# Weight sums of the third projection pair moved to VectorE, and the projection work reordered, in a DeltaNet layer step

## The reference, cut to what matters

```python
h = rmsnorm(x, norm1_g) * (1 + scale1) + shift1
proj = h @ w_in                       # columns: pool, q, k, v, gate, beta, alpha, merge
qkv = silu(short_conv(proj[..., OFF_Q:OFF_G], conv_w))   # 5 taps, depthwise
q, k = l2norm(q) * DN_HEAD_DIM ** -0.5, l2norm(k)
o_f, s_f = gated_delta_chunked(q, k, v, beta_f, g_f, s0_f)     # 8 heads of 128
o_b, s_b = gated_delta_chunked(flip(q), flip(k), ...)          # the other direction
o = rms(o_f + flip(o_b)) * onorm_g * silu(gate)
x = x + gate1 * ((merge_a * a_out + merge_b * (o @ dn_proj)) @ w_out)
```

## Time and profile before

| | us |
|---|---|
| median of 3 runs | 2573.36 (2573.13 to 2573.65) |
| profiled execution, its own time | 2571.28 |
| its span in the profile | 2569.5 |
| prologue, up to `scan_done` of L1377 | 129.8 |
| eight heads, up to the last L1358 | 129.8 to 1353.1 |
| output projection, routing and experts | 1353.1 to 2569.5 |

### The profile page before, as it was taken

One profiled execution on the slowest core, in us unless ns is written; L12 is line 12 of the kernel. 1 busy time (PEld: TensorE's weight loads), 2 busy tenths in 40 slices (PEclk: granted clock), 3 DMA queues, 4 the chain that ended last, 5 costly groups with the idle time before them and its releaser, 6 DMA issues.

```text
span 2569.5 us, 39903 instructions
## 1 busy us (share of the span) xinstructions
PE 2370.0 (92%) x14256; PEld 1718.9 (67%) x14256; DVE 1122.5 (44%) x2133; ACT 943.5 (37%) x2447; POOL 440.5 (17%) x295
## 2 busy tenths in 40 slices
PE   6889899898989989897999999959999999999998
PEld 3456556465655556565564444549999999999996
DVE  2657585765758576674623531770100100010013
ACT  3154555536455553644431113312223223222313
POOL 0222231322323132232310000000110011011000
PEclk8989999999999999998999999979999999999999
DMA  9610202011010201102224332266788788878874
GB/s 325 233 44 20 65 26 73 17 39 58 21 65 25 74 17 39 44 10 65 68 94 173 112 130 98 91 220 217 237 285 300 251 276 289 292 239 287 298 246 157
DMA packets 198401, 361.05 MB, mean 141 GB/s; under 512 B 8954, under 2 KB 72327, under 8 KB 195243
## 3 DMA queue, kind: packets, MB, share of 16 engines
q1 hardware_dynamic: 192139, 341.77, 38.0%
q0 software_dynamic: 6176, 18.29, 2.8%
HBM read 319.97 MB, written 40.06 MB: 140 GB/s over the span
## 4 chain that ended last, share of the span: by engine, by line
PE 52%; DVE 2%; issue 1%; DMA 1%; ACT 1%; POOL 0%; SPq 0%; DVEq 0%; ACTq 0%; POOLq 0%
PE bank L2373 20%; PE bank L2387 10%; PE bank L2002 5%; PE bank L1739 4%; PE bank L729 3%; PE bank L1757 2%; PE bank L710 1%; PE bank L2011 1%; PE bank L2345 1%; PE bank L2355 1%; PE bank L926 0%; PE bank L718 0%; DMA arena<-in_w_in 0%; PE bank L2413 0%; PE bank L995 0%
## 5 line engine op out<-in xcount | busy, mean ns | idle before, releaser
L729 PE MATMUL bank<-arena 128*128 128x512 f32 x1344 | 697.4, 622 | 21.6 <-ACT arena L763 21.6
L2373 PE MATMUL bank<-arena 128*128 128x144 f32 x4096 | 512.9, 286 | 3.1 <-ACT arena L2421 3.1
L2373 PEld LDWEIGHTS bank<-arena 128*128 128x128 f32 x4096 | 509.6, 190 | 3.2 <-ACT arena L2421 3.2
L2488 DVE TENSOR_TENSOR arena<-arena,bank 128x144 f32<-128x144 f32 x128 | 39.1, 306 | 698.2 <-ACT arena L2435 698.2
L729 PEld LDWEIGHTS bank<-arena 128*128 128x128 f32 x1344 | 221.9, 195 | 119.4 <-issue 95.0
L2387 PE MATMUL bank<-arena 128*128 128x144 f32 x2048 | 257.3, 286 | 0.7 <-DVE arena L2488 0.7
L2387 PEld LDWEIGHTS bank<-arena 128*128 128x128 f32 x2048 | 253.8, 189 | 1.9 <-DVE arena L2488 0.9
L1101 ACT ACTIVATE arena<-bank 128x384 f16<-128x384 f16 (+1 forms) x360 | 163.7, 492 | 215.1 <-PE bank L918 118.4
L2435 ACT ACTIVATE arena<-bank 128x144 f32<-128x144 f32 x128 | 37.4, 292 | 464.3 <-PE bank L2373 464.3
L926 PEld LDWEIGHTS bank<-arena 128*128 128x128 f16 x1296 | 98.7, 98 | 149.8 <-issue 127.4
L1186 DVE SCALAR_TENSOR_TENSOR arena<-arena 128x1156 f32<-128x1156 f32 x96 | 143.1, 1490 | 0.3
(11 more groups left out here) (311 smaller groups left out, 3185.2 us busy)
## 6 DMA issues: line engine op xcount, KB each, us to landing
arena<-in_exp_w_gate SPq DMA_DIRECT2D x32, 2048.0 KB, 10.1
arena<-in_exp_w_up SPq DMA_DIRECT2D x32, 2048.0 KB, 14.9
arena<-in_exp_w_down SPq DMA_DIRECT2D x32, 2048.0 KB, 10.8
arena<-in_w_in SPq DMA_DIRECT2D x52, 512.0 KB, 5.2
arena<-in_ada_w SPq DMA_DIRECT2D x24, 1024.0 KB, 7.9
side_dram<-arena SPq DMA_DIRECT2D x20, 576.0 KB, 5.7
arena<-g_dram SPq DMA_DIRECT2D x16, 576.0 KB, 4.3
arena<-in_x_sample SPq DMA_DIRECT2D x16, 512.0 KB, 7.1
```

What stands on the lines that cost most here:

```text
L729: ins = nc.tensor.matmul(bank[:, 0:LH], w[:, k, :], x[:, k, :], start=(k == 0 and job[2] in "127"), stop=(k == KH - 1), skip_group_check=( ...
L2373: last = nc.tensor.matmul(banks[3 + f % 2][:, m * CAP:(m + 1) * CAP], w_unit[2 * half + m][:, k, col:col + P], xsT[:, k, :], start=(k == 0 ...
```

## The change

- **Order of the jobs in the loop**: the context jobs of qv and kg come first (qvc0, qvc1, kgc0, kgc1), then the other seven of qv, the other seven of kg, then AB as before. In the last head job g2 moves from before CD to between CD and EF, and the DMA of `w_dn[0]`, which waits for g2, moves behind the waits for CD3 on SyncE.
- **Units of fill**: "start" 5 to 4; "Y20", "Y21", "Y22" from 1.5, 1.5, 1 to 1, 0.5, 0.5; the last group's product place in the first three levels (P2_2, P4_2, P8_2) 1 to 0; "fix" 3 to 4; "end1" 4 to 5.5. With the sum of the rest in "end2", 14.25 units follow the last scan step where 9.25 did. In the last head only the three places P2_2, P4_2, P8_2 change, to 0.
- **ScalarE** copies the jobs of "start" between the SiLU of q and that of v, ahead of the table load and of the wait for `scan_done`.
- **GpSimd** makes, right behind `scan_done`, the sums 1, 2 of qv, 1, 2, 4 of kg and 3 of qv and kg, then the masks L1427 and L1434, then sum 4 of qv. The kg sums have space of their own (`w_sum2`, over part of the masks and prologue tables), so they needn't wait for qv's jobs.
- **VectorE** makes the four AB sums of the seven loop heads in the scan: two behind the tap of chunk 2, one in chunk 4, one in chunk 7. In the last head GpSimd makes them.
- **Taps**: order v, q, k in place of q, v, k. Levels 4 and 8 have none now; one each stays in levels 16, 32, 64; 12 lie in the scan (10 before), with two in chunk 3 and one behind the state of chunk 5.
- **Prologue**: the last token sum `h_sum3` on GpSimd waits for `scan_done`; TensorE no longer waits for it.

```diff
-        ORDER = pair_jobs("qv") + pair_jobs("kg") + pair_jobs("AB")
-        ORDER_LAST = pair_jobs("AB") + ("g0", "g1", "g2") + pair_jobs("CD") + pair_jobs("EF")
+        (QV_C, QV_X), (KG_C, KG_X) = split("qv"), split("kg")
+        ORDER = QV_C + KG_C + QV_X + KG_X + pair_jobs("AB")
+        ORDER_LAST = pair_jobs("AB") + ("g0", "g1") + pair_jobs("CD") + ("g2",) + pair_jobs("EF")
...
-        FILL = {"start": 5, "nk": 2.75, "qT": 4, "kk": 4, "Y20": 1.5, "Y21": 1.5, "Y22": 1, "X0": 1, "X1": 1, "X2": 1, "res": 2, "fix": 3, "end1": 4}
-        FILL |= {f"{x}{b}_{g}": 1 for b in LEVELS for x in "ZP" for g in range(3)}
+        FILL = {"start": 4, "nk": 2.75, "qT": 4, "kk": 4, "Y20": 1, "Y21": 0.5, "Y22": 0.5, "X0": 1, "X1": 1, "X2": 1, "res": 2, "fix": 4, "end1": 5.5}
+        FILL |= {f"{x}{b}_{g}": 0 if b in LEVELS[:3] and (x, g) == ("P", 2) else 1 for b in LEVELS for x in "ZP" for g in range(3)}
...
             silu(1)
             silu(0)
+            evac("start")
             silu(2)
             act.preload_act_table_set(LN_EXP)
             act.wait_ge(sem("scan_done"), h + 1)
-            evac("start")
...
+            def sums_fourth(pair):
+                one, to = weights_of(pair[0]), sums_of(pair)
+                if pair != "kg":
+                    eng.wait_ge(sem("pj_filled"), job_at(h, order, pair + "2"))
+                sum_out(pair + "4", to[2], one[:, KH:KD, :], to[1], ALU.subtract)
...
-                if not last_h and lv > 0:
-                    conv_tap(dve, h + 1, 0, lv - 1)
+                if lv >= 3:
+                    tap()
...
+            sums_first, sums_third, sums_fourth = sum_steps(dve, nc.vector, h, order)
+            tap()
             remainder(1)
             tap()
             state(0)
...
             for t in range(2, NT):
                 remainder(t)
                 tap()
+                if t == 3:
+                    tap()
                 add(f"scan{t}b")
+                if t == 2 and not last_h:
+                    sums_first("AB")
+                elif t == 4 and not last_h:
+                    sums_third("AB")
+                elif t == 7 and not last_h:
+                    sums_fourth("AB")
                 state(t)
-            if not last_h:
-                conv_tap(dve, h + 1, 1, TAPS - 1)
+                if t == 5:
+                    tap()
...
             pool.wait_ge(sem("scan_done"), h + 1)
-            sums_first(first, len(FIRST) + len(ORDER) * h)
-            sums_third(first)
-            sums_fourth(first)
+            pool.wait_ge(sem("pj_filled"), len(FIRST) + len(ORDER) * h)
+            if last_h:
+                sums_first("AB")
+                gate_sums()
+                sums_third("AB")
+            else:
+                sums_first("qv")
+                sums_first("kg")
+                sums_fourth("kg")
+                sums_third("qv")
+                sums_third("kg")
...
+            sums_fourth("AB" if last_h else "qv")
+            all_drained(pool, h, 1, "kq")
+            for d in range(2):
+                low_part(d)
+                attention(d)
             if last_h:
...
+                for pair, used in (("CD", "AB5"), ("EF", "CD5")):
+                    pool.wait_ge(sem("pj_filled"), job_at(h, order, used))
+                    sums_first(pair)
+                    sums_third(pair)
+                    sums_fourth(pair)
...
             pool.wait_ge(sem("pj_filled"), len(FIRST))
+            pool.wait_ge(sem("scan_done"), 1)
             nc.gpsimd.tensor_tensor(h_sum3, h22, h12, ALU.subtract).then_inc(sem("sums_ready"), 1)
...
             pe_gate2(pe)
-            pe.wait_ge(sem("sums_ready"), H_SUMS)
```

More of the change, by code:

```diff
@@ L127, in build @@
         masks_f = mask_words.rearrange("p (s l c) -> p s l c", s=2, l=7)
+        silu_c = take(KD * (P // 4))
+        tab_words = take(9 * NT * 2 * H)
+        tab = {n: tab_words[:, i * NT * 2 * H:(i + 1) * NT * 2 * H].rearrange("p (t d) -> p t d", t=NT)
+               for i, n in enumerate(("g", "gc", "tmp", "tmp2", "beta", "gcb", "ndec", "kd", "dl"))}
         row_bits, row_moves = take(8), take(8)
@@ L679, in weights_wait, with summed_at, sums_of @@
                 eng.wait_ge(sem(f"w_side_in{x % 2}"), 16 * (h + 1 + x // 2))
-        H_SUMS, W_SUMS = 4, 12
-        def sums_before(h, order, job):
-            pairs = [n for n in order if n[-2:] == "c1"]
-            mine = [n for n in pairs if n[:2] == job[:2]]
-            extra = 2 if order is ORDER_LAST and job[:2] in ("CD", "EF") else 0
-            return H_SUMS + W_SUMS * h + 4 * pairs.index(mine[0]) + extra
+        H_SUMS = 4
+        SUMS = ("qv1", "qv2", "kg1", "kg2", "kg4", "qv3", "kg3", "qv4", "AB1", "AB2", "AB3", "AB4")
+        SUMS_LAST = ("AB1", "AB2", "g1", "g2", "AB3", "AB4", "CD1", "CD2", "CD3", "CD4", "EF1", "EF2", "EF3", "EF4")
+        def summed_at(h, order, name):
+            return H_SUMS + len(SUMS) * h + (SUMS_LAST if order is ORDER_LAST else SUMS).index(name) + 1
+        def sums_of(pair):
+            one = weights_of(pair[0])
+            return w_sum2 if pair == "kg" else w_sum + [one[:, KH:KD, :]]
         def project(pe, h, order):
@@ L1169, in conv_tap @@
         def conv_tap(dve, h, j, tap):
+            first = isinstance(h, int) and h == 0
+            turn = (CONV_TURN_FIRST if first else CONV_TURN).index(j)
             if tap == 0:
-                if isinstance(h, int) and h == 0:
+                if first:
                     dve.wait_ge(sem("pj_drained"), copied_at(0, FIRST, ("q2", "k2", "v2")[j]))
@@ L1187, in conv_tap, with sum_steps, sum_out, sums_first @@
             ins.then_inc(sem("tap_done" if tap < TAPS - 1 else "conv_done"), 1)
+        def sum_steps(eng, unit, h, order):
+            def sum_out(name, out, x, y, op):
+                if name[-1] in "24":
+                    eng.wait_ge(sem("sums_ready"), summed_at(h, order, name[:2] + {"2": "1", "4": "2"}[name[-1]]))
+                unit.tensor_tensor(out, x, y, op).then_inc(sem("sums_ready"), 1)
+            def sums_first(pair):
+                for name in pair:
+                    weights_wait(eng, h, order, name)
+                one, two, to = weights_of(pair[0]), weights_of(pair[1]), sums_of(pair)
+                sum_out(pair + "1", to[0], two[:, 0:KH, :], two[:, KH:KD, :], ALU.add)
+                sum_out(pair + "2", to[1], to[0], one[:, 0:KH, :], ALU.subtract)
+            def sums_third(pair):
+                one, two = weights_of(pair[0]), weights_of(pair[1])
+                eng.wait_ge(sem("pj_filled"), job_at(h, order, pair + "c1"))
+                sum_out(pair + "3", two[:, 0:KH, :], one[:, 0:KH, :], two[:, 0:KH, :], ALU.subtract)
+            def sums_fourth(pair):
[3 more added lines that the diff above has]
+                sum_out(pair + "4", to[2], one[:, KH:KD, :], to[1], ALU.subtract)
+            return sums_first, sums_third, sums_fourth
         def body_dve(dve, h, last_h=False):
@@ L1199, in add, with tap @@
                 added[0] = to
+            taps = [(j, tap) for j in (2, 0, 1) for tap in range(TAPS)]
+            def tap():
+                if not last_h:
+                    conv_tap(dve, h + 1, *taps.pop(0))
             def decay_arguments(d):
```

81 lines of the change are left out of this document (21 added, 60 removed).

## The result

| | before | after |
|---|---|---|
| median | 2573.24 us | 2435.72 us (2434.98 to 2440.75) |
| profiled execution, and its span | 2571.28, 2569.5 | 2440.75, 2439.0 |
| prologue, up to `scan_done` | 129.8 | 129.0 |
| first head | 152.4 | 137.6 |
| six loop heads, mean | 150.1 | 132.7 |

The ratio is 0.9472 (95% interval 0.9456 to 0.9488): 137.5 us less in the median, 130.5 in the profiled executions. The forecast was 92. All but 1 us of it lies in the eight heads. (The profiled execution of after is its longest; a later one of the same kernel has a span of 2435.0.)

What follows compares the result with a forecast made beforehand. TensorE, busy 92% of the span, was taken as the bound. Per loop head 15.2 us gained less 3.9 is 11.3, by six 67.8; with 13.4 (first head) and 11 (last), 92 us less: 2481 us, range 2453 to 2530.

Steps and rivals of the forecast that it cites:

- The X_init wait and the slow steps behind it: TensorE at the triangle start: 5.6 us of wait and 2.8 of slow steps go per loop head, a 1.0 rest stays.
- The lock at the k norm: VectorE's k norm could stand behind the last of GpSimd's seven sums, costing TensorE at most 0.7 us a head.
- The bank wait at the start: Head's start: TensorE's 3.1 us wait for ScalarE's copy of a bank goes, plus 1.8 us of slow work behind it.
- The output wait: Behind the last scan step: the wait for the normed output, 1.3 + 0.6 us, goes because 14.25 units cover it.
- Copies and norms: Head's start: new waits for kgc0's bank copy and k's transposes cost 0 to 2.5 us per loop head, taken as 1.2.
- The levels: Less cover against no GpSimd kg and AB sums there: net -1.5 to +4 us cost per loop head, taken as +0.7.
- The scan: Four sums and two more taps on VectorE overrun some chunks: 0 to 5.6 us cost per loop head, taken as 1.0.
- First head: Head 0 gains 13.4 us, including 2.4 from prologue taps no longer meeting `h_sum3`, less 3.9 of new costs.
- the price of 3.9: New costs per head, in us: X_init rest 1.0, copies and norms 1.2, levels 0.7, scan 1.0.
- Last head: Gains 17.6 less 6.3, taken as 11 us; EF weight wait goes, about 2.4 us of GpSimd wait comes in level 64.
- The third: Rival: without GpSimd sums the levels' short waits go too, and no X_init rest; 3.2 us more by 8, 2455; chance 0.13.
- The second: Rival: cover taken from the levels is missed, VectorE bounds the first three; 6.5 us gained a head, 2519; chance 0.27.

Runs made afterwards that it cites:

- b_masks: Kernel before, with only GpSimd's fourth qv sum moved behind the masks in the seven loop heads: 2524.92 us, ratio 0.9815.
- a_old_fill: Changed kernel with the old amounts of side work (fill) between the steps restored: 2434.13 us, ratio 0.9465.
- a_kg_levels: Changed kernel with GpSimd's four k and g weight sums put back between the steps of the levels in the loop heads: 2461.29 us, ratio 0.9572.
- a_pool_ab: Changed kernel with the four AB sums of the loop heads back on GpSimd, behind the second attention: 2450.55 us, ratio 0.9526.
- b_taps: Kernel before with only the convolution's q taps moved from levels 4 and 8 to two places in the scan: 2560.25 us, ratio 0.9956.
- b_ kernels: The follow-up kernels made from the kernel before, with one or two parts of the change: 2524.92, 2546.09, 2498.27 and 2560.25 us.
- b_both: Kernel before with two moves, the fourth qv sum behind the masks and ScalarE's start copies ahead of the SiLU of v: 2498.27 us, ratio 0.9712.

## Why the prediction was wrong, step by step

The direction held, and so did the mechanisms ahead of the levels; the size did not, because in the levels the forecast had the sign wrong: 137.5 us gained where 92 were forecast, 17 us below the low end of the range. Against the steps:

- *The X_init wait and the slow steps behind it* (5.6 + 2.8, less a rest of 1.0): right. The wait is 0.84 us, the steps run at full speed, and b_masks shows 6.6 us for the one sum alone. The lock at the k norm, which the prediction priced at up to 0.7, fell the other way round: the products of the k norm ran undisturbed, and it was the seventh sum that lasted 2.28 us at 408.71.
- *The bank wait at the start* (3.1 + 1.8): right, 3.3 by the copy alone and the rest with the shorter start.
- *The output wait* (1.3 + 0.6) is gone, but for another reason than the longer cover: a_old_fill, with the old cover, waits only 0.17 us for the normed output (0.63 behind it stays). The traces show what shortened that chain. In before the last tap runs beside GpSimd's sum of the outputs; a_old_fill has no tap there, and the sum is 1.14 us shorter:

```profile
420.25 1.42 DVE L1186 SCALAR_TENSOR_TENSOR arena<-arena 128x1156 f32<-128x1156 f32 x1
420.38 3.76 POOL L1472 TENSOR_TENSOR arena<-arena 128x1152 f32<-128x1152 f32 x1 [16.08 <-ACT arena L1140]
```

```profile
383.48 2.62 POOL L1501 TENSOR_TENSOR arena<-arena 128x1152 f32<-128x1152 f32 x1 [53.27 <-ACT arena L1156]
```

The sum lasts 3.76 us in all seven loop heads of before and of every kernel made from it, and 2.62 in their last head, which has no taps, and in all heads of after and of every kernel made from that. So 1.15 of the 1.32 us came from the moved tap and the rest from the cover.
- *Copies and norms* (1.2 to pay): nothing was paid in the loop heads: the wait list has no such row there. It was paid once, in the first head, where the k transposes waited 2.12 us (L919 for L1266) and ran slower behind it (3.85 us against 2.13).
- **The levels** (0.7 to pay, bound -1.5 to +4): the step that failed. They gave 3.3 us, outside the bound. I had the row that shows the mechanism and applied it to the taps alone. The copies of the levels are the same case, two tiles in SBUF beside a GpSimd sum, and TensorE waits for some of them. Undone singly, the k and g sums cost 3.0 us a head (a_kg_levels), the A and B sums 1.7, of which 1.4 are listed waits (a_pool_ab), and in before the taps 1.4 in the levels (b_taps). Against these stand 2.1 us that the missing cover costs there (a_old_fill): 5.35 - 2.1 = 3.3. So cover was a real price, and a forecast of the levels had to set it against 5.35 us, not against one tap. VectorE's 42.03 busy us in the old levels held the answer: they fell by 5.9, of which the two taps are 2.2.
- *The scan* (1.0 to pay): 0.1. I summed the overruns of single chunks, 1.6 us, as if TensorE had to wait for each; its fill covered them. The sums took 0.68 us each on VectorE, as said.
- *First head* 13.3 for 13.4, which is partly luck: the prologue ended 0.8 us earlier, not 2.4 (in the b_ kernels, which leave it as it is, it ends between 128.7 and 132.0), and the price of 3.9 came as 2.1 us of wait and 1.7 of slow work at the k transposes. *Last head* 12.6 for 11. The new wait of 2.4 us for GpSimd in level 64 came as said, at 1142.97; the weights of A and B were waited for 5.78 us, and the EF wait is gone.
- *The rivals.* The third, with its short waits, was the right one in kind and given 0.13. It forecast 2455, still 19 us too slow: it booked the 3.2 us of waits but kept the forecast's costs of the copies, the levels and the scan. The second, to which I gave 0.27, drew on the same waits and read them the wrong way: that TensorE waits 43 times for VectorE was taken as a lack of cover. More cover does hide such waits (a_old_fill), but what made most of them was VectorE held by GpSimd.

Sum per loop head: ahead of the levels 10.3 us (b_both) and 3.9 more, where b_both still has waits of 1.3 and 0.6 at the output, 1.1 for the bank and 1.0 for VectorE's add; in the levels 5.35 less 2.1; in the scan -0.1. That is 17.4. The parts undone singly in the levels make 3.0 + 1.7 + 1.4 = 6.1, not 5.35 (5.0 without the context steps): two of them were undone in after, which has less cover, so they are no exact split. A kernel of before with no sums in its levels was not run.

## What to carry to other kernels

When TensorE waits often and briefly for VectorE, look at what GpSimd does at that moment before asking for more cover: compare the same instruction with and without a GpSimd operation under way (0.55 against 1.2 to 1.6 us here), and count every VectorE instruction of that kind, not just the one on which it was first seen. A queue that stands in a wait charges all that is behind it; two calls moved out of such places gave half of this change. The operation that a queue runs late can also be the one held: here a tap made GpSimd's sum of the outputs 1.14 us longer and TensorE waited for it.

## What the runs showed of the hardware

- The predicated copies are held beside a GpSimd sum like the two-source arithmetic of the earlier trace rows, and GpSimd is held as well: L1211 lasted 2.28 us at 408.71, beside the k norm's product of two SBUF tiles (1.22 us from 408.64), and 1.27 alone; the sum of the outputs 3.76 us beside a tap and 2.62 alone. Four sums of some 1.35 us in the levels cost TensorE 3.0 us a head.
- A write of 128x512 f32 on GpSimd takes 0.52 us and slows no copy.
- A predicated copy whose data lie in a bank is untouched beside a sum (0.55 us). A VectorE operation on one SBUF tile and a column is not: L1206 takes 0.28 us alone and 1.0 to 1.4 beside a sum, so that nine in after, beside six sums, took 6.59 us (L1259 from 401.39).
- The waits cost more than they last: behind the 5.58 us for `X_init` the granted clock is 0.50, the lower level, from 614.59 to 619.20, and four records take 3.93 us. Over a head it is 0.97 with that wait, 1.00 without.
